# A two-layer decoder trunk in f32: new order of the first product and of the work at the boundaries between sublayers

## The chip, the cores and the metric

The kernel runs on one core of one Trainium2 chip. The metric is the device time of one execution in microseconds, the median of several runs.

## The reference

The input h is a residual stream of 256 tokens by 1024 channels in float32. Each of two layers computes, in this order (all weights float32):

```
f = swiglu(rms(h) @ ffn1_w_gu) @ ffn1_w_down;  h += 0.5 * rms(f)
u = rms(h) @ w_in                 # 5120 columns: q, k, v of two mixers, and two gates
h += rms((sigmoid(g1) * (stick_breaking(u) @ w1) + sigmoid(g2) * (differential(u) @ w2)) @ w_out)
f = swiglu(rms(h) @ ffn2_w_gu) @ ffn2_w_down;  h += 0.5 * rms(f)
e = (p[i] @ w_ple_proj) * sigmoid(rms(h) @ w_ple_gate);  h += rms(e)
```

rms(...) is a norm over the channels with a gain of its own each time. The hidden width of the FFNs is 2816; p[i] is 256 tokens by 256. The output has float32 accuracy, so each product is made of several reduced-precision ones.

## The kernel before, in words

**Units and splits.** The weights come in units of 2048 columns by 128 rows (1 MB). A unit is two halves of 1024 columns or four quarters of 512. `raw`, `w_hi` and `w_lo` hold three units each (three slots, unit u in slot u mod 3). SP loads a unit into `raw` as soon as VectorE has split the unit that was there. ScalarE rounds it to the fast format, with the norm's gain (`high`, line 646, also 643 and 657: `w_hi`). VectorE takes the rest (`low`, line 1084, also 1081, 1062, 1065 and in quarters 1098: `w_lo`). Every product is then three matmuls (`exact`, lines 1473 to 1475): high x high, low weights, low inputs. The inputs are split the same way: TensorE turns 128 tokens by 512 channels of h into a PSUM bank (`turn`, line 1520, four transposes), ScalarE copies the high part (`high_inputs`, line 677), VectorE the low part (`low_inputs`, line 1109).

**Tiles and order.** Tokens come in two tiles of 128 (t = 0, 1). `by_tiles` works two units in the order: unit u tile 0, unit u+1 tile 0, unit u tile 1, unit u+1 tile 1. A turn is put between two quarters of such a product; `before` is a table of what goes in front of quarter k. In `wide` products a quarter is 128 input channels by 512 output columns. In `deep` products quarter (n, k) is output columns n and input channels k, so the order over a unit's quarters is 0, 2, 1, 3.

**Boundaries.** Three times per layer (`boundary`, q = 1 before w_in, q = 3 before the second FFN, q = 4 before the gate) the last product of a sublayer ends, its squares are summed by ScalarE (`square_post`, line 694), GpSimd makes 1/sqrt of the mean (line 536 and `r_post`, line 538), VectorE multiplies by the gain (`gained`, line 1185) and adds to h (`update_h`, line 1198), each tile by halves of 512 channels. h is then turned and split for the next product. Beside this, both engines split the units that are used next: `next_unit` is unit u+1 of the coming pair, `unit_after` is unit u+2. All engines execute in order, so what stands ahead of a wait and what stands behind it is set by these two functions, one for ScalarE and one for VectorE. At the boundary TensorE first works unit u for tile 0, then the first quarter of unit u+1 for tile 0, then turns the first half of h's tile 1, then goes on; the turn of the second half stands in unit u for tile 1. Before unit u+1 it waits for all of the unit (`begin`).

**The opening.** The first product is p times the projection (unit 0), four pieces of 256 KB. Pieces 1 and 3 are loaded by SP, pieces 0 and 2 by ScalarE's queue, which then loads two quarters of x; the two others (indices 1 and 3) are issued by ScalarE between its splits (`load_x`). SP's queue begins with p's tile 0, piece 1, p's tile 1, piece 3, and then the pieces of units 1 to 3. TensorE runs 13 transposes of the identity (`warm_up`, line 1884), turns p's tile 0 (line 1877), runs 5 more, and begins `proj`.

Of the kernel before, what the change touches and what calls it, by code (L numbers as in the profile page):

```python
# [60 lines left out]
PIECED = 4  # L61
WARM_UP = (13, 5)
MEANS = 20
# [13 lines left out]
def trunk_kernel(nc, a, out):  # L77
    with ExitStack() as ctx:
# [9 lines left out]
        def bank(b):  # L88
            return ps[:, b, :]
# [257 lines left out]

        def p_bank(i):
            return bank(P_BANK if i else FIRST_P_BANK).rearrange("p (k n) -> p k n", k=2)

# [267 lines left out]
        def _(act):  # L618
# [41 lines left out]
            def high_p(i, t=0, toks=slice(0, SEQ)):  # L660

                act.wait_ge(p_turned, nth_p(i, t))
                act.activation(p_hi[:, :, toks], p_bank(i)[:, :, toks], ACT.Copy).then_inc(p_high, 1)

# [32 lines left out]
            def boundary(i, n, q, pairs, next_unit, unit_after):  # L697


                square_post(i, n, pair(pairs[0]), 0)  # L700
                next_unit(0)
                high_inputs(i, q, 0)
                next_unit(1)
                square_post(i, n, pair(pairs[1]), 1)
                unit_after()
                high_inputs(i, q, 1, (0,))
                square_pre(i, n + 1, 0)
                high_inputs(i, q, 1, (1,))
                square_pre(i, n + 1, 1)
# [216 lines left out]
            for i in range(DEPTH):  # L926
                def loads():
                    load_post(i, "ffn1_post_g", 0, 0)
                    load_post(i, "mix_post_g", 0, 1)
                    if i == 0:  # L930
# [7 lines left out]
                boundary(i, 0, 1, DOWN_PAIR,  # L938
                         lambda n: high(i, U_WIN + 1, 12, halves=(n,)), lambda: high(i, U_WIN + 2, 8))

# [5 lines left out]
                boundary(i, 1, 3, OUT_PAIR,  # L946
                         lambda n: high(i, U_FFN2 + 1, 20, halves=(n,)), lambda: high(i, U_FFN2 + 2, 16))

# [8 lines left out]
                if i < LAST:  # L957
                    high_p(i + 1)
                boundary(i, 2, 4, DOWN_PAIR,
                         lambda n: high(i, U_GATE + 1, 26, ks=2, halves=(n,)), lambda: high(i, U_GATE + 2, 28, ks=2))  # L960
                high(i, U_GATE + 3, 30, ks=2)
# [55 lines left out]
        def _(dve):  # L1017
# [351 lines left out]
            def low_p(i, t=0, toks=slice(0, SEQ)):  # L1369

                dve.wait_ge(p_high, nth_p(i, t))
                dve.tensor_tensor(p_lo[:, :, toks], p_bank(i)[:, :, toks], p_hi[:, :, toks].bitcast(F32),
                                  ALU.subtract).then_inc(p_split, 1)

            low_piece(U_PROJ, 0)
            low_p(0, 0, slice(0, P))
            low_piece(U_PROJ, 1)
            low_piece(U_PROJ, 2)
            low_p(0, 1, slice(P, SEQ))
            low_piece(U_PROJ, 3)  # L1380
            keep_first_gain()
# [88 lines left out]
        def _(pe):  # L1470
# [104 lines left out]
            def ffn(i, f, q, u0, before_last):  # L1575
# [85 lines left out]
                if (i, f) == (0, 0):  # L1661
                    for s in range(2):
                        for t in range(TT):
                            before = turned_at(0, 0, (1, 3)[t:t + 1], (1,)) if s == 0 else {}
                            if t == 0:
                                before = {k: pieced(u0 + s, k, before.get(k)) for k in range(4)}
                            mm = first_gate_up(s, t, before)
                            if s == 1 and t == 0:
                                mm.then_inc(gu_done, 1)
                        mm.then_inc(units_used, 1)  # L1670
                else:
                    second = turned_at(i, q, (2,), (1,))
                    if q == 0:
                        second[0] = lambda: pe.wait_ge(half_split, i)
                        second[2] = lambda: begin(i, u0 + 1)
                    by_tiles(i, u0, first_gate_up, gu_done, {(1, 0): second, (0, 1): turned_at(i, q, (3,), (1,))},
                             own_wait=(1,) if q == 0 else ())
                step(1, 1, first=True)
# [141 lines left out]
            def mixer(i):  # L1820
# [7 lines left out]
                def w_out(u, s, t, before):  # L1828
# [3 lines left out]

                by_tiles(i, U_WIN, first_win, win_done, {(1, 0): turned_at(i, 1, (2,), (1,)),
                                                         (0, 1): turned_at(i, 1, (3,), (1,))})
                for m in range(2, 20):
# [37 lines left out]
            def turn_p(i, tiles=range(TT)):  # L1873
                pe.wait_ge(p_in[tiles[0]], 16 * i + 16)
                for k in range(2):
                    for t in tiles:
                        mm = pe.transpose(p_bank(i)[:, k, t * P:(t + 1) * P], p_nat[:, t, k * P:(k + 1) * P],
                                          ident[:, :])
                mm.then_inc(p_turned, 1)
# [11 lines left out]
            def turn_gains():  # L1891
# [4 lines left out]
                pe.transpose(bank(GAIN_BANK[1])[:, 0:66], g_rows[0:66, :], ident[0:66, 0:66]).then_inc(cols_turned, 1)  # L1896

            def proj(i):

                if i:  # L1900
                    begin(i, U_PROJ)
                for t in range(TT):
                    pe.wait_ge(p_split, nth_p(i, t))
                    if i:
                        pe.wait_ge(ple_sig, 2 * i - 1 + t)
                        before = turned_at(i, 0, (0, 1), (1, 2)) if t == 0 else None
                    elif t == 0:
                        turns = {1: lambda: turn_p(0, (1,)), **turned_at(0, 0, (0,), (3,))}
                        before = {k: pieced(U_PROJ, k, turns.get(k)) for k in range(4)}
                    else:  # L1910
                        before = {0: turn_first_gain, **turned_at(0, 0, (2,), (2,)), 3: turn_gains}
# [7 lines left out]
            turn_p(0, (0,))  # L1919
            warm_up(WARM_UP[1])  # L1920
            for i in range(DEPTH):
                proj(i)
                ffn(i, 0, 0, U_FFN1, lambda: None)
# [4 lines left out]
                def gate(u, s, t, before):  # L1928
# [4 lines left out]
                by_tiles(i, U_GATE, lambda s, t, before: gate(0, s, t, before), None,  # L1933
                         {(1, 0): turned_at(i, 4, (2,), (1,)), (0, 1): turned_at(i, 4, (3,), (2,))})
                by_tiles(i, U_GATE + 2, lambda s, t, before: gate(2, s, t, before))
# [23 lines left out]
```

## Time and profile before

| | before |
|---|---|
| runs, us | 1187.34, 1187.6, 1187.7 (median 1187.6) |
| profiled execution, us | 1187.24 |
| its span, us | 1185.2 |
| TensorE matmul busy | 1173.8 us, 99% |
| VectorE, ScalarE, GpSimd busy | 72%, 61%, 8% |
| loaded from memory | 215 MB, 182 GB/s over the span |
| mean granted TensorE clock | 0.999 |

The span runs from the first to the last instruction; the execution's own time lies 2.0 us above it. Busy times of TensorE overlap, since a matmul's start is given exactly and its end is modelled: two matmuls of 512 columns start 0.23 us apart and are shown with 0.39 us each. So a gap of TensorE is best read from the starts. A row of the timeline gives start, duration, engine, line, operation, output and inputs, shape and count, and in brackets the idle time before it and what ended that.

### The profile page before, as it was taken

What the parts mean: (1) busy time and instruction counts of PE and PEld (TensorE: products, weight loads), DVE (VectorE), ACT (ScalarE), POOL (GpSimd) and SP (SyncE); (2) the same over time, 40 slices, a digit from 0 to 9 for tenths busy, and PEclk for the clock granted to TensorE, in tenths of its full rate; (3) what the DMA queues carried; (4) which work ended last, traced back from release to release, by engine and by line L of the source; (5) the groups of instructions that cost most, each with busy time, mean ns of one, the idle gap of its engine ahead of it and who ended that gap; (6) DMA issues with size and microseconds to landing.
All of it is one profiled execution on the core that took longest, in us unless ns stands there. A gap on an engine that the chain in (4) does not pass through costs nothing.

```text
span 1185.2 us, 17137 instructions
## 1 busy us (share of the span) xinstructions
PE 1173.8 (99%) x6013; PEld 984.4 (83%) x6013; DVE 848.7 (72%) x1235; ACT 719.9 (61%) x1163; POOL 92.9 (8%) x157
## 2 busy tenths in 40 slices
PE   8999999999999999999999999999999999999997
PEld 7888888888788888888888888888877888888886
DVE  5766777588667866676787776676976776767666
ACT  6655556666665755564685655576656666555555
POOL 4000000042000100000110000010600010000002
PEclk9999999999999999999999999999999999999999
DMA  8656565553345555556546565756343456556550
GB/s 269 232 183 201 171 218 192 198 178 118 132 178 178 178 196 194 191 172 230 178 158 203 175 209 178 249 162 208 114 159 133 169 178 213 175 179 206 183 196 36
DMA packets 138654, 215.36 MB, mean 182 GB/s; under 512 B 6958, under 2 KB 97904, under 8 KB 138608
## 3 DMA queue, kind: packets, MB, share of 16 engines
q1 hardware_dynamic: 135808, 208.43, 52.9%
q10 hardware_dynamic: 2576, 6.29, 1.6%
q8 instruction: 28, 0.46, 0.2%
q14 instruction: 18, 0.15, 0.0%
q0 software_dynamic: 224, 0.04, 0.0%
HBM read 213.68 MB, written 1.05 MB: 181 GB/s over the span
## 4 chain that ended last, share of the span: by engine, by line
PE 96%; ACT 2%; DVE 1%; DMA 1%; issue 0%; POOL 0%; SPq 0%; DVEq 0%; POOLq 0%; ACTq 0%
PE ps L1591 22%; PE ps L1473 19%; PE ps L1475 19%; PE ps L1474 19%; PE ps L1601 12%; PE ps L1520 2%; PE ps L1692 1%; DMA raw<-in_w_ple_proj 1%; PE ps L1723 1%; DVE w_lo L1084 0%; ACT w_hi L646 0%; PE ps L1736 0%; PE ps L1709 0%; ACT prob L804 0%; PE ps L1752 0%
## 5 line engine op out<-in xcount | busy, mean ns | idle before, releaser
L1084 DVE SCALAR_TENSOR_TENSOR w_lo<-raw,g_layer,w_hi 128x512 fp32r<-128x512 f32 (+1 forms) x504 | 369.6, 793 | 131.4 <-ACT w_hi L646 131.4
L646 ACT ACTIVATE w_hi<-raw,g_layer 128x512 fp32r<-128x512 f32 (+1 forms) x524 | 346.9, 732 | 113.5 <-PE ps L1601 97.0
L1591 PE MATMUL ps<-x_both,w_hi 128*128 128x512 f32 x1152 | 287.7, 392 | 0.0
L1473 PE MATMUL ps<-w_hi,x_both 128*128 128x512 f32 x640 | 257.4, 402 | 0.0
L1475 PE MATMUL ps<-w_hi,x_both 128*128 128x512 f32 x640 | 250.2, 391 | 0.0
L1474 PE MATMUL ps<-w_lo,x_both 128*128 128x512 f32 x640 | 249.6, 390 | 0.0
L1591 PEld LDWEIGHTS ps<-x_both,w_hi 128*128 128x128 f32 x1152 | 209.4, 189 | 39.3 <-issue 0.3
L1081 DVE TENSOR_TENSOR w_lo<-raw,w_hi 128x1024 fp32r<-128x1024 f32 x114 | 134.7, 1221 | 55.0 <-ACT w_hi L643 55.0
L643 ACT ACTIVATE w_hi<-raw 128x1024 fp32r<-128x1024 f32 x114 | 114.7, 1052 | 91.7 <-PE ps L1475 91.6
L1601 PEld LDWEIGHTS ps<-x_both,w_lo 128*128 128x128 f32 x1152 | 152.6, 191 | 8.4
L1601 PE MATMUL ps<-x_both,w_lo 128*128 128x256 f32 x1152 | 156.0, 283 | 0.0
L1473 PEld LDWEIGHTS ps<-w_hi,x_both 128*128 128x128 f32 x640 | 120.2, 188 | 27.1 <-issue 3.3
L1475 PEld LDWEIGHTS ps<-w_hi,x_both 128*128 128x128 f32 x640 | 120.1, 188 | 26.1
L1474 PEld LDWEIGHTS ps<-w_lo,x_both 128*128 128x128 f32 x640 | 120.4, 188 | 22.8
L1473 PE MATMUL ps<-w_hi,ht_hi 128*128 128x512 f32 x320 | 124.9, 390 | 0.0
L1475 PE MATMUL ps<-w_hi,ht_lo 128*128 128x512 f32 x320 | 124.6, 389 | 0.0
L1474 PE MATMUL ps<-w_lo,ht_hi 128*128 128x512 f32 x320 | 124.5, 389 | 0.0
L728 ACT ACTIVATE glu<-glu 128x512 f32<-128x512 f32 x36 | 22.8, 633 | 78.5 <-DVE glu L1130 78.5
L1475 PEld LDWEIGHTS ps<-w_hi,ht_lo 128*128 128x128 f32 x320 | 60.1, 188 | 12.5
L1474 PEld LDWEIGHTS ps<-w_lo,ht_hi 128*128 128x128 f32 x320 | 60.1, 188 | 12.4
L1473 PEld LDWEIGHTS ps<-w_hi,ht_hi 128*128 128x128 f32 x320 | 60.1, 188 | 12.3
L536 POOL TENSOR_TENSOR ms_post<-mean_post,eps_half 128x1 f32<-128x1 f32 x8 | 2.4, 305 | 548.6 <-ACT tmp L694 548.6
(217 smaller groups left out, 1008.7 us busy)
## 6 DMA issues: line engine op xcount, KB each, us to landing
raw<-in_ffn_w_gu SPq DMA_DIRECT2D x170, 512.0 KB, 4.6
raw<-in_ffn_w_down SPq DMA_DIRECT2D x88, 512.0 KB, 4.0
raw<-in_w_in SPq DMA_DIRECT2D x80, 512.0 KB, 4.6
raw<-in_w_out SPq DMA_DIRECT2D x16, 512.0 KB, 3.7
raw<-in_w_ple_gate SPq DMA_DIRECT2D x16, 512.0 KB, 4.1
raw<-in_w_branch_sb SPq DMA_DIRECT2D x8, 512.0 KB, 3.7
raw<-in_w_branch_diff SPq DMA_DIRECT2D x8, 512.0 KB, 3.7
raw<-in_ffn_w_gu SPq DMA_DIRECT2D x12, 256.0 KB, 7.6
```

The costliest lines, as they stand in the source:

```text
L643: last = act.activation(w_hi[:, s, part], raw[:, s, part], ACT.Copy)
L646: last = act.activation(w_hi[:, s, part], raw[:, s, part], ACT.Copy, scale=g_layer[:, g:g + 1])
L728: act.activation(glu_g, glu_g, ACT.Silu).then_inc(silu_done, 2)
L1081: last = dve.tensor_tensor(w_lo[:, s, part], raw[:, s, part], whi[:, part], ALU.subtract)
L1084: last = dve.scalar_tensor_tensor(out=w_lo[:, s, part], in0=raw[:, s, part], scalar=g_layer[:, g:g + 1], in1=whi[:, part], op0=ALU.mult, o ...
L1473: pe.matmul(dst, x_h, w_h, start=first, stop=False, **group)
L1474: pe.matmul(dst, x_h, w_l, start=False, stop=False, **group)
L1475: return pe.matmul(dst, x_l, w_h, start=False, stop=last, **group)
L1520: mm = pe.transpose(x_bank(i, q, idx)[:, k * P:(k + 1) * P], src[:, (4 * n + k) * P:(4 * n + k + 1) * P], ident[:, :])
L1591: mm = pe.matmul(dst, w_hi[:, s, cols], x_both[:, :, 4 * half + k, :], start=half == 0 and k == 0, stop=stop and k == 3, skip_group_check= ...
L1601: mm = pe.matmul(bank(FLAT_BANK[j])[:, 0:SEQ], w_lo[:, s, cols], x_hi[:, 4 * half + k, :], start=False, stop=False, skip_group_check=True)
L1692: mm = pe.transpose(dst[:, k * SEQ + t * P:k * SEQ + (t + 1) * P], src[:, t, k * P:(k + 1) * P], ident[:, :])
```

## The change

It has two parts.

In the opening, p's tile 1 is loaded second on SP's queue. TensorE turns both tiles of p before the first product, with 3 transposes in place of 5 between them, and each tile has a PSUM bank of its own. The product goes through the pieces in the order 0, 2 for tile 0, 0, 2 for tile 1, then 1, 3 and 1, 3; ScalarE and VectorE split in the order piece 0, p's tile 0, piece 2, p's tile 1, piece 1, piece 3.

At the three boundaries, ScalarE sums the squares of tile 1 ahead of the second half of `next_unit`, and does `unit_after` by halves. VectorE updates the first half of tile 1 of h ahead of the last two quarters of `next_unit`, and the second half of h behind the low part of the first half of x. Where the product is `deep` (ks = 2), the quarters of `next_unit` are split in the order 0, 2, 1, 3. TensorE waits for the first two split quarters before unit u+1 and for the rest before its third quarter.

```diff
-WARM_UP = (13, 5)
+WARM_UP = (13, 3)
...
-        HT_BANK, P_BANK, FIRST_P_BANK = 6, 7, 3
+        HT_BANK, P_BANK, FIRST_P_BANK = 6, 7, (3, 5)
...
-            load_p(0)
+            for t in range(TT):
+                load_p(t)
...
-            load_pieces(U_PROJ, (1,))
-            load_p(1)
-            load_pieces(U_PROJ, (3,))
+            load_pieces(U_PROJ, (1, 3))
...
@@ ScalarE, boundary @@
                 next_unit(0)
                 high_inputs(i, q, 0)
+                square_post(i, n, pair(pairs[1]), 1)
                 next_unit(1)
-                square_post(i, n, pair(pairs[1]), 1)
-                unit_after()
+                unit_after(0)
                 high_inputs(i, q, 1, (0,))
                 square_pre(i, n + 1, 0)
+                unit_after(1)
                 high_inputs(i, q, 1, (1,))
                 square_pre(i, n + 1, 1)
...
@@ ScalarE, opening @@
             high_p(0, 0, slice(0, P))
+            high_piece(U_PROJ, 2)
+            high_p(0, 1, slice(P, SEQ))
             high_piece(U_PROJ, 1)
-            high_p(0, 1, slice(P, SEQ))
-            high_piece(U_PROJ, 2)
             high_piece(U_PROJ, 3)
             load_x(1)
...
@@ VectorE @@
-            def low_quarter(i, u, gain, ks, k):
-
+            def low_quarter(i, u, gain, ks, n):
+
+                k = n if ks == 4 else (0, 2, 1, 3)[n]
                 s, part = slot(u), slice(k * W, (k + 1) * W)
-                if k % 2 == 0:
-                    dve.wait_ge(hi_ready, 2 * UNITS * i + 2 * u + k // 2 + 1)
+                dve.wait_ge(hi_ready, 2 * UNITS * i + 2 * u + k // 2 + 1)
...
-                if k == 3:
+                if n == 1:
+                    ins.then_inc(half_split, 1)
+                if n == 3:
                     ins.then_inc(split_done, 1)
...
                 for k in range(2):
                     next_unit(k)
                     low_inputs(i, q, 0, (k,))
+                wait_gained(i, n, 1)
+                gained(i, n, pair(pairs[1]), 1, 0)
+                update_h(i, n, 1, 0)
                 for k in range(2, 4):
                     next_unit(k)
-                wait_gained(i, n, 1)
-                for k in range(2):
-                    gained(i, n, pair(pairs[1]), 1, k)
-                    update_h(i, n, 1, k)
+                gained(i, n, pair(pairs[1]), 1, 1)
                 low_inputs(i, q, 1, (0,))
+                update_h(i, n, 1, 1)
                 unit_after()
                 low_inputs(i, q, 1, (1,))
...
@@ TensorE @@
+            def by_halves(i, q, u, second):
+
+                second[0] = lambda: pe.wait_ge(half_split, 4 * i + (0, 1, None, 2, 3)[q])
+                second[2] = lambda: begin(i, u + 1)
+                return second
...
+            def first_proj():
+
+                beside = {(0, 1): lambda: (turn(0, 0, 0), turn_first_gain()), (0, 3): lambda: turn(0, 0, 2),
+                          (1, 3): turn_gains}
+                for t, k in ((0, 0), (0, 2), (1, 0), (1, 2), (0, 1), (0, 3), (1, 1), (1, 3)):
+                    if (t, k) in beside:
+                        beside[t, k]()
+                    if k == 0:
+                        pe.wait_ge(p_split, nth_p(0, t))
+                    if t == 0 and k < 3:
+                        pe.wait_ge(piece_split, (0, 2, 1).index(k) + 1)
+                    if (t, k) == (0, 3):
+                        begin(0, U_PROJ)
...
             warm_up(WARM_UP[0])
             turn_p(0, (0,))
             warm_up(WARM_UP[1])
+            turn_p(0, (1,))
+            first_proj()
             for i in range(DEPTH):
-                proj(i)
+                if i:
+                    proj(i)
```

## Rows read from the trace of the kernel before

**Rows 1.** The page, chain of work that ended last, by engine.

```profile
PE 96%; ACT 2%; DVE 1%; DMA 1%; issue 0%; POOL 0%; SPq 0%; DVEq 0%; POOLq 0%; ACTq 0%
```

**Rows 2.** Waits, TensorE's weight loads: us in total, times, longest.

```profile
PEld ps L1520 <- DVE h L1198: 3.1, 11, 0.4
```

**Rows 3.** Timeline, TensorE at the boundary to the second FFN: start, us, what.

```profile
384.93 0.40 PE L1475 MATMUL ps<-w_hi,x_both 128*128 128x512 f32 x1
...
388.35 0.39 PE L1475 MATMUL ps<-w_hi,x_both 128*128 128x512 f32 x1
388.76 0.66 PE L1520 MATMUL ps<-ident,h 128*128 128x128 f32 x4
...
394.56 0.39 PE L1473 MATMUL ps<-w_hi,x_both 128*128 128x512 f32 x1
```

**Rows 4.** Timeline, TensorE at the boundary to the gate.

```profile
570.73 0.39 PE L1475 MATMUL ps<-w_hi,x_both 128*128 128x512 f32 x1
...
573.70 0.39 PE L1473 MATMUL ps<-w_hi,x_both 128*128 128x512 f32 x1
...
574.38 0.65 PE L1520 MATMUL ps<-ident,h 128*128 128x128 f32 x4
```

**Rows 5.** Windows: stretch, its length, busy PE, PEld, DVE, ACT, POOL, clock, DMA, GB/s.

```profile
5.50:10.00 4.50, 2.80 (x13) 1.56 (x12) 2.14 (x4) 2.00 (x4) 3.17 (x17) 1.00 1.04 333
```

**Rows 6.** DMA issues at 0.80, 1.25, 1.72, 2.19 and 9.54: us to landing last.

```profile
soft<-in_p SPq DMA_DIRECT2D x1, 128.0 KB, 2.9
...
raw<-in_w_ple_proj ACTq DMA_DIRECT2D x1, 256.0 KB, 5.1
...
soft<-in_p SPq DMA_DIRECT2D x1, 128.0 KB, 5.5
...
raw<-in_w_ple_proj SPq DMA_DIRECT2D x1, 256.0 KB, 7.3
...
h<-in_x ACTq DMA_DIRECT2D x1, 256.0 KB, 5.8
```

**Rows 7.** Timeline, ScalarE in the opening, projection piece 3.

```profile
9.54 0.63 ACT L657 ACTIVATE w_hi<-raw 128x512 fp32r<-128x512 f32 x1 [0.68 <-DMA raw<-in_w_ple_proj]
```

**Rows 8.** Timeline, TensorE in the opening.

```profile
1.59 3.04 PE L1884 MATMUL ps<-ident 128*128 128x128 f32 x13 [1.59 <-POOL ident L474]
...
5.99 0.50 PE L1473 MATMUL ps<-w_hi,p_hi 128*128 128x512 f32 x1
...
6.55 0.40 PE L1475 MATMUL ps<-w_hi,p_lo 128*128 128x512 f32 x1
...
15.92 0.39 PE L1473 MATMUL ps<-w_hi,x_both 128*128 128x512 f32 x1
...
16.61 0.60 PE L1520 MATMUL ps<-ident,h 128*128 128x128 f32 x4
```

**Rows 9.** Timeline, VectorE, ScalarE and GpSimd at the boundary to the second FFN.

```profile
385.82 1.41 DVE L1098 SCALAR_TENSOR_TENSOR w_lo<-raw,g_layer,w_hi 128x512 fp32r<-128x512 f32 x2
...
387.95 0.75 DVE L1198 SCALAR_TENSOR_TENSOR h<-tmp,r_post,h 128x512 f32<-128x512 f32 x1
...
393.34 0.69 DVE L1109 TENSOR_TENSOR x_both<-ps,x_both 128x512 fp32r<-128x512 f32 x1
...
385.69 1.02 ACT L694 ACTIVATE tmp<-ps 128x1024 f32<-128x1024 f32 x1
386.59 0.20 ACT L694 ACTIVATION_READ_ACCUMULATOR tmp<-ps 128x1 f32 x1
...
387.36 0.56 POOL L538 TENSOR_TENSOR r_post<-ms_post,neg_half 128x1 f32<-128x1 f32 x1
```

**Rows 10.** Timeline, VectorE and ScalarE at the boundary to the gate.

```profile
570.12 0.75 DVE L1098 SCALAR_TENSOR_TENSOR w_lo<-raw,g_layer,w_hi 128x512 fp32r<-128x512 f32 x1
...
570.26 1.14 ACT L646 ACTIVATE w_hi<-raw,g_layer 128x1024 fp32r<-128x1024 f32 x1
571.31 1.01 ACT L694 ACTIVATE tmp<-ps 128x1024 f32<-128x1024 f32 x1
```

More of the change, by code:

```diff
@@ L346, in trunk_kernel, with p_bank @@
         X_FIRST_BANK = (0, 0, 1, 1)
-        def p_bank(i):
-            return bank(P_BANK if i else FIRST_P_BANK).rearrange("p (k n) -> p k n", k=2)
+        def p_bank(i, t=0):
+            return bank(P_BANK if i else FIRST_P_BANK[t]).rearrange("p (k n) -> p k n", k=2)
         def nth_p(i, t):
@@ L662, in high_p @@
                 act.wait_ge(p_turned, nth_p(i, t))
-                act.activation(p_hi[:, :, toks], p_bank(i)[:, :, toks], ACT.Copy).then_inc(p_high, 1)
+                act.activation(p_hi[:, :, toks], p_bank(i, t)[:, :, toks], ACT.Copy).then_inc(p_high, 1)
             def keep_e(i, t):
@@ L938, in _ @@
                 boundary(i, 0, 1, DOWN_PAIR,
-                         lambda n: high(i, U_WIN + 1, 12, halves=(n,)), lambda: high(i, U_WIN + 2, 8))
+                         lambda n: high(i, U_WIN + 1, 12, halves=(n,)), lambda n: high(i, U_WIN + 2, 8, halves=(n,)))
                 load_post(i, "ffn2_post_g", 1, 0)
@@ L946, in _ @@
                 boundary(i, 1, 3, OUT_PAIR,
-                         lambda n: high(i, U_FFN2 + 1, 20, halves=(n,)), lambda: high(i, U_FFN2 + 2, 16))
+                         lambda n: high(i, U_FFN2 + 1, 20, halves=(n,)),
+                         lambda n: high(i, U_FFN2 + 2, 16, halves=(n,)))
                 act.preload_act_table_set("silu_and_others")
@@ L959, in _ @@
                 boundary(i, 2, 4, DOWN_PAIR,
-                         lambda n: high(i, U_GATE + 1, 26, ks=2, halves=(n,)), lambda: high(i, U_GATE + 2, 28, ks=2))
+                         lambda n: high(i, U_GATE + 1, 26, ks=2, halves=(n,)),
+                         lambda n: high(i, U_GATE + 2, 28, ks=2, halves=(n,)))
                 high(i, U_GATE + 3, 30, ks=2)
@@ L1371, in low_p @@
                 dve.wait_ge(p_high, nth_p(i, t))
-                dve.tensor_tensor(p_lo[:, :, toks], p_bank(i)[:, :, toks], p_hi[:, :, toks].bitcast(F32),
+                dve.tensor_tensor(p_lo[:, :, toks], p_bank(i, t)[:, :, toks], p_hi[:, :, toks].bitcast(F32),
                                   ALU.subtract).then_inc(p_split, 1)
@@ L1376, in _ @@
             low_p(0, 0, slice(0, P))
-            low_piece(U_PROJ, 1)
             low_piece(U_PROJ, 2)
             low_p(0, 1, slice(P, SEQ))
+            low_piece(U_PROJ, 1)
             low_piece(U_PROJ, 3)
@@ L1671, in ffn @@
                 else:
[L1672 to L1675, printed above, removed]
+                    second = by_halves(i, q, u0, turned_at(i, q, (2,), (1,)))
                     by_tiles(i, u0, first_gate_up, gu_done, {(1, 0): second, (0, 1): turned_at(i, q, (3,), (1,))},
-                             own_wait=(1,) if q == 0 else ())
+                             own_wait=(1,))
                 step(1, 1, first=True)
@@ L1831, in w_out @@
                                 u + s == 0, u + s == 3, before)
-                by_tiles(i, U_WIN, first_win, win_done, {(1, 0): turned_at(i, 1, (2,), (1,)),
-                                                         (0, 1): turned_at(i, 1, (3,), (1,))})
+                by_tiles(i, U_WIN, first_win, win_done, {(1, 0): by_halves(i, 1, U_WIN, turned_at(i, 1, (2,), (1,))),
+                                                         (0, 1): turned_at(i, 1, (3,), (1,))}, own_wait=(1,))
                 for m in range(2, 20):
@@ L1876, in turn_p @@
                     for t in tiles:
-                        mm = pe.transpose(p_bank(i)[:, k, t * P:(t + 1) * P], p_nat[:, t, k * P:(k + 1) * P],
+                        mm = pe.transpose(p_bank(i, t)[:, k, t * P:(t + 1) * P], p_nat[:, t, k * P:(k + 1) * P],
                                           ident[:, :])
@@ L1896, in turn_gains @@
                 pe.transpose(bank(GAIN_BANK[1])[:, 0:66], g_rows[0:66, :], ident[0:66, 0:66]).then_inc(cols_turned, 1)
+            def first_proj():
[10 more added lines that the diff above has]
+                        begin(0, U_PROJ)
+                    cols, toks = piece(U_PROJ, k), slice(t * P, (t + 1) * P)
+                    mm = exact(bank(E_PAIR[t] + k // 2), p_hi[:, k % 2, toks], p_lo[:, k % 2, toks],
+                               w_hi[:, slot(U_PROJ), cols], w_lo[:, slot(U_PROJ), cols], k % 2 == 0, k % 2 == 1)
+                    if (t, k) == (0, 3):
+                        mm.then_inc(e_done, 1)
+                mm.then_inc(units_used, 1)
             def proj(i):
-                if i:
-                    begin(i, U_PROJ)
+                begin(i, U_PROJ)
                 for t in range(TT):
                     pe.wait_ge(p_split, nth_p(i, t))
[L1904 to L1911, printed above, removed]
+                    pe.wait_ge(ple_sig, 2 * i - 1 + t)
+                    before = turned_at(i, 0, (0, 1), (1, 2)) if t == 0 else None
                     mm = deep(slot(U_PROJ), E_PAIR[t], p_hi, p_lo, 0, t, True, True, before)
@@ L1933, in _ @@
                 by_tiles(i, U_GATE, lambda s, t, before: gate(0, s, t, before), None,
-                         {(1, 0): turned_at(i, 4, (2,), (1,)), (0, 1): turned_at(i, 4, (3,), (2,))})
+                         {(1, 0): by_halves(i, 4, U_GATE, turned_at(i, 4, (2,), (1,))),
+                          (0, 1): turned_at(i, 4, (3,), (2,))}, own_wait=(1,))
                 by_tiles(i, U_GATE + 2, lambda s, t, before: gate(2, s, t, before))
```

## The prediction

> **What bounds the kernel now.** I read the page first: TensorE's matmuls hold 96% of the chain that ended last, all other engines together 4% [rows 1]. So an edit is worth only what it does to TensorE's gaps. The list of waits says how little there is to win at the boundaries: the transposes of h (L1520) waited 3.1 us in all over 11 cases, on the weight-load side, where the matmul before hides part of it [rows 2]. The array itself loses less. From 384.93 to 388.35 it makes 15 matmuls, 0.228 us apart; the turn of h then starts at 388.76, 0.41 later, so 0.18 us is lost, and some 0.06 more for restarting [rows 3]. At the gate boundary the turn comes 0.23 x 3 behind 573.70, so only the restart is lost [rows 4]. Four boundaries of the first kind and two of the second hold at most 4 x 0.24 + 2 x 0.07 = 1.1 us. The opening holds more: between 5.5 and 10 us TensorE is busy for 2.80 us of 4.50 [rows 5].
>
> The profiled execution is 1187.24 us around a span of 1185.2; the median of the three runs is 1187.6, so I add 0.36 at the end. A difference under 0.2% (2.4 us) can't be told from none.
>
> **The opening.** Removed: two warm-up transposes. Moved: p's second load from third to second place on SP's queue, so projection piece 1 goes behind it; piece 2's split ahead of piece 1's on ScalarE and VectorE; TensorE turns p's tile 1 before any product and then works pieces 0 and 2 for both tiles before 1 and 3. No instruction is added.
> Landings: p's first tile lands 2.9 us after its issue at 0.80, the second 5.5 after 1.72 (7.2); piece 2 5.1 after 1.25 (6.4), piece 3 7.3 after 2.19 (9.5), x's second half 5.8 after 9.54 (15.3) [rows 6]. p's tile 1 will be issued at 1.26. It lands no earlier than the first (3.7) and no later than its old time, with more bytes ahead (7.2); it's nearest to the first, 128 KB behind it, so I take 4.5. TensorE reaches it at 5.4, behind 13 warm-ups, p's tile 0 and 3 more, in the place of the two that go. Piece 1 takes p's old place in the bytes, 7.2.
> Chain: ScalarE splits piece 2 at 6.4 (0.63 us a piece), p's tile 1 (about 0.4) at 7.0, piece 1 at 7.3, piece 3 at 9.54 as now, since DMA sets that one [rows 7]; VectorE follows each with 0.69, what it needs for another 128x512 subtraction [rows 9]: piece 2 done at 7.8, p at 8.1, piece 1 at 8.8, piece 3 at 10.9 as now. TensorE: first product at 5.99 as now [rows 8], wait to 7.8, then three quarters of three matmuls (0.23 each, 0.69) to 10.0; x's first turn (0.35) and the gain's; quarter 1 from 10.55, another turn, quarter 3 at 11.7 (its weights 10.9, not late), quarters 1 and 3 of tile 1, end 14.0. Now the first matmul on x starts at 15.92 [rows 8]: 1.9 us earlier.
> What is late next: the turn of x's second half. TensorE comes to it at 14.0 + 0.69 = 14.7, and the data land at 15.3, because ScalarE issues that load behind piece 3's split, which hasn't moved. Now this turn stands at 16.61 [rows 8]; it will stand at 15.4. So 0.7 of the 1.9 us turns into a new wait and **the opening gives 1.2 us**. Behind it ScalarE's and VectorE's splits follow TensorE's turns and shift with them. Bounds: 0.4 (piece 2 or p's tile 1 late by 0.8) to 1.9 (the load no hindrance).
> The clock: the first 13 warm-ups take 3.04 us, 0.23 each; x's four transposes later take 0.60, 0.15 each [rows 8]. So the array was at the lower of its two levels (1.2 GHz) at first, at 2.4 later, and as many transposes stand before the first product after the change as now: I price this at 0. The Trainium skill, TensorE: Matmul & The Clock Gate, Part 4 (PE-mode transpose), says that a transpose doesn't count as activity that brings the full clock. By that rule the products would open at the low clock, before and after alike, for the same sum. The trace disagrees: behind transposes alone, the first product takes 0.56 us from its first matmul at 5.99 to its third at 6.55, two steps that at half the rate would take 0.9 [rows 8].
>
> **The four wide boundaries** (to w_in and to the second gate-up, twice each; same code and shapes). I work out the one at 388. ScalarE now squares tile 1 (385.69) behind the second half of the next unit's split. Squaring moves ahead of that half, but it waits for TensorE's last product, whose last matmul starts at 384.93 and lasts 0.40 [rows 3]: it starts at 385.4, and 1.1 us later the squares are there, 386.5 against 386.79. GpSimd adds 1.13, to r_post's end: 387.6 against 387.92 [rows 9]. h's first half gets its update (0.75) at 387.65, done 388.4, and TensorE's turn goes at 388.58 without a gap: 0.24 gained.
> The price is VectorE's order. Today it fills the time until the squares are there with quarters 2 and 3 (385.82, 1.41 us) [rows 9]. After the change these stand behind the update, so it idles from 385.8 to 386.5 and, with one 0.68 product between, from 387.2 to 387.65. Then: quarters 2 and 3 to 389.75, against TensorE's need at 389.7 (0.09 lost); product 0.68; x's low part of tile 1, first half, done 391.0, needed 391.2; update of h's second half 391.7, needed 391.9; both just in time. Then the whole of the unit after (four quarters, 2.65 us with overlap) to 394.25, and only behind it the low part of tile 1's second half, done 394.95, now 393.34 + 0.69 = 394.03 [rows 9]. TensorE needs it where it now starts that product, 394.56 [rows 3], less 0.24 plus 0.09 = 394.4. That is a new stall of 0.55 us. **Net +0.4 each, +1.7 in all.** The split of the unit after is not halved on VectorE, so ScalarE's halving buys nothing. Bounds: -0.24 (no stall) to +0.9 (all of the lateness).
>
> **The two gate boundaries.** There the product wants quarters 0 and 2 first, and the new order of the quarters gives it them. But quarter 2 lies in the second half of the unit, whose high part ScalarE now makes behind the squares. Before: half at 570.26 (1.14 us), squares at 571.31 [rows 10]. After: the squares wait for the last matmul (570.73 + 0.39 [rows 4]), start 571.18, the next instruction 0.99 later: half from 572.17 to 573.3. VectorE, in order, has quarter 2 where quarter 1 stands at 570.12 [rows 10], at the head of its queue; it idles until 573.35, and behind it stand x's low part, product and update of tile 1. Quarter 2 is done at 574.1 (0.75), TensorE wants it at 573.70 [rows 4]: 0.45 lost. Then x's low part (0.62 step), product (0.72), update (0.75) end at 576.1: the turn goes at 576.2 instead of 574.38. Then quarters 1 and 3 end at 577.5, wanted at 577.4. From there VectorE has everything in time. **+1.9 to +2.0 each, +3.9 in all.** Lower bound -0.07, no stall; upper +2.6, should the low part of tile 1 also come late.
> Later stages: the unit after is split, by the same counting, about 3 us ahead of its need. Its slots in raw come free up to 5 us later, and SP's loads behind them; each has the whole of two units' products, some 11 us, to land in 4 to 5. TensorE has no idle time further on that could absorb the shift, so it is carried to the end.
>
> **Sum.** -1.2 + 1.7 + 3.9 = +4.4 us on 1187.24: 1191.6, with 0.36 for the median 1192.0.
>
> **The rivals.**
> (a) As above, 70%: own range 1190.4 to 1193.4.
> (b) The wide boundaries don't stall, because the ten steps of VectorE between 385.8 and 394.95 are 0.55 us shorter than I add them up. Then 4 x -0.24 instead of +1.7: 1189.3. Against it: each step is read from a row, and all would have to be 6% short. 14%.
> (c) The clock, place: 5.4 to 6 us. If p's tile 1 still lands near 7.2, TensorE idles in front of the first product with two warm-ups fewer, and the products start at the low clock: 24 matmuls at 0.43 (512 columns at half the rate of 0.228) are 4.8 us more, less what waits hide, some 3: 1195. For it: the old landing; against: fewer bytes ahead. The page above would have the low clock without late data. 4%.
> (d) Faster: the gate unit's second half isn't late. It decides at VectorE's quarter 2: were the half high by 571.4 as now, quarter 2, product and update would fit before 574.4; and if likewise at the wide boundaries, with nothing lost to the order, all 1.1 is gained and the opening's 1.2 to 1.9: 1184.6 to 1185.3. The order written out for ScalarE speaks against it. 5%.
> (e) The change doesn't do what it says in the opening: a late piece eats the 1.2, so 1193.2. 7%.
>
> **How the numbers follow.** (a) and (b) are 84%; the range from 1189.2 to 1193.8 takes in both and (e). Slower by over 0.2% begins at 1190.0: all of (a), (c), (e) and a bit of (b): 0.82. Faster, under 1185.2: 0.04. The rest 0.14.
>
> **What would show it.** TensorE's list of waits gets entries on VectorE's low part of x at four boundaries (0.5 each), and at two gates on h's update (1.3 each) and on quarter 2 (0.45 each); ScalarE's second half of the gate unit starts behind the squares; the first matmul on x stands near 14.0, and the turn behind it waits for the load of x. I'm wrong if TensorE shows no idle of a microsecond near 575, or if the opening's turn of x's second half goes before 15.

## The result and the profile after

The changed kernel takes 1191.18 us (median of 8 runs, 1190.6 to 1191.48) beside 1187.39 us for the kernel before (8 runs): the ratio is 1.0031, 95% interval 1.002 to 1.0042. It is slower by 3.8 us. The profiled execution took 1191.3 us around a span of 1189.2, which is 4.0 more than before, so its trace can be read for nearly the whole difference of the medians.

The page of the changed kernel, chain of work that ended last, by engine:

```profile
PE 92%; DVE 4%; ACT 2%; DMA 1%; issue 1%; POOL 0%; SPq 0%; DVEq 0%; POOLq 0%; ACTq 0%
```

In [rows 1] VectorE had 1% of this chain and TensorE 96%. The chain now leaves TensorE more often. The waits of the changed kernel say where, first TensorE's matmuls, then its weight loads (us in total, times, longest; the line of a turn is now L1525, that of the first of three matmuls L1478):

```profile
PE ps L1525 <- DVE h L1202: 2.1, 2, 1.0
...
PE ps L1525 <- DMA h<-in_x: 1.6, 1, 1.6
PE ps L1478 <- DVE w_lo L1100: 0.8, 2, 0.4
PE ps L1478 <- DVE x_both L1113: 0.7, 4, 0.2
...
PEld ps L1525 <- DVE h L1202: 3.8, 7, 1.5
...
PEld ps L1478 <- DVE x_both L1113: 2.4, 4, 0.6
```

The first four lines are the waits of the matmuls: two waits on h's update (the gates), one on the load of x (the opening), two on a split quarter (the gates), four on the low part of x (the wide boundaries). None of them was in the matmuls' list of before. In [rows 2] the weight loads' waits on h were 11 short ones; here 2 of the 7 make up most of the sum.

To see how much each cost, I set the starts of the same turns in both traces side by side. A turn's shift is its start after minus its start before, and the step is the shift less that of the row above. So the step of a row is what the stretch between the two turns cost; the cost of a boundary, which falls behind its first turn, stands in the row below it. (In the opening, "x's second half" is channels 512 to 1023 of tile 0, and "x's last half" the same channels of tile 1.)

| turn | start before | shift | step |
|---|---|---|---|
| x's second half, in the opening | 16.61 | -1.10 | -1.10 |
| first turn at the boundary to w_in | 198.17 | -1.05 | +0.05 |
| first turn at the boundary to FFN 2 | 382.20 | -0.80 | +0.25 |
| first turn at the gate boundary | 568.00 | -0.57 | +0.23 |
| first turn behind the gate, layer 1 | 594.43 | +1.54 | +2.11 |
| boundary to w_in, layer 2 | 782.65 | +1.56 | +0.02 |
| boundary to FFN 2, layer 2 | 966.66 | +1.79 | +0.23 |
| gate boundary, layer 2 | 1151.99 | +2.01 | +0.22 |
| last turn of that boundary | 1162.30 | +4.10 | +2.09 |

So the opening gave 1.05, each wide boundary cost 0.22 to 0.25, each gate 2.1, and everything between them next to nothing: -1.05 + 0.93 + 4.20 = +4.1.

**The gate.** Timeline of the changed kernel: ScalarE, then VectorE, then TensorE, to be set beside [rows 4, 10]:

```profile
570.60 1.03 ACT L693 ACTIVATE tmp<-ps 128x1024 f32<-128x1024 f32 x1 [0.79 <-PE ps L1480]
571.52 0.19 ACT L693 ACTIVATION_READ_ACCUMULATOR tmp<-ps 128x1 f32 x1
571.61 2.18 ACT L645 ACTIVATE w_hi<-raw,g_layer 128x1024 fp32r<-128x1024 f32 x2
...
572.79 0.75 DVE L1100 SCALAR_TENSOR_TENSOR w_lo<-raw,g_layer,w_hi 128x512 fp32r<-128x512 f32 x1 [3.15 <-ACT w_hi L645]
573.46 0.68 DVE L1113 TENSOR_TENSOR x_both<-ps,x_both 128x512 fp32r<-128x512 f32 x1
574.06 0.68 DVE L1189 TENSOR_TENSOR tmp<-ps,post_g 128x512 f32<-128x512 f32 x1
574.84 0.75 DVE L1202 SCALAR_TENSOR_TENSOR h<-tmp,r_post,h 128x512 f32<-128x512 f32 x1
...
573.68 0.47 PE L1478 MATMUL ps<-w_hi,x_both 128*128 128x512 f32 x1 [0.40 <-DVE w_lo L1100]
...
575.65 0.66 PE L1525 MATMUL ps<-ident,h 128*128 128x128 f32 x4 [1.03 <-DVE h L1202]
```

ScalarE idles 0.79 us for TensorE's last product, sums the squares and only then makes the second half (571.61). In VectorE's order nothing stands ahead of quarter 2 that it could do, so it idles 3.15 us; the three steps queued behind it end at 575.6, and the turn of h goes 0.06 later. The last matmul before the turn had started at 574.22.

**A wide boundary** (to the second FFN), VectorE, GpSimd, TensorE of the changed kernel, beside [rows 3, 9]. This boundary starts 0.80 us earlier than before:

```profile
385.77 0.69 DVE L1189 TENSOR_TENSOR tmp<-ps,post_g 128x512 f32<-128x512 f32 x1 [0.81 <-ACT tmp L693]
386.60 0.75 DVE L1202 SCALAR_TENSOR_TENSOR h<-tmp,r_post,h 128x512 f32<-128x512 f32 x1
387.27 1.41 DVE L1100 SCALAR_TENSOR_TENSOR w_lo<-raw,g_layer,w_hi 128x512 fp32r<-128x512 f32 x2
...
390.45 2.73 DVE L1086 SCALAR_TENSOR_TENSOR w_lo<-raw,g_layer,w_hi 128x512 fp32r<-128x512 f32 x4
393.11 0.68 DVE L1113 TENSOR_TENSOR x_both<-ps,x_both 128x512 fp32r<-128x512 f32 x1
...
385.74 0.19 POOL L535 TENSOR_TENSOR ms_post<-mean_post,eps_norm 128x1 f32<-128x1 f32 x1 [5.54 <-ACT tmp L693]
386.01 0.55 POOL L537 TENSOR_TENSOR r_post<-ms_post,neg_half 128x1 f32<-128x1 f32 x1
...
387.55 0.39 PE L1480 MATMUL ps<-w_hi,x_both 128*128 128x512 f32 x1
387.78 0.60 PE L1525 MATMUL ps<-ident,h 128*128 128x128 f32 x4
...
393.28 0.39 PE L1480 MATMUL ps<-w_hi,x_both 128*128 128x512 f32 x1
393.85 0.50 PE L1478 MATMUL ps<-w_hi,x_both 128*128 128x512 f32 x1 [0.18 <-DVE x_both L1113]
```

The turn now follows the matmul by the usual 0.23 (387.55 to 387.78), where it was 0.41. But the low part of x starts at 393.11, behind four quarters of the unit after, ends at 393.79, and TensorE's step from 393.28 to 393.85 is 0.57, 0.34 too long, with some 0.1 more for restarting.

**The opening**, TensorE and ScalarE of the changed kernel, beside [rows 7, 8]:

```profile
5.82 0.50 PE L1478 MATMUL ps<-w_hi,p_hi 128*128 128x512 f32 x1 [0.39 <-DVE p_lo L1377]
...
13.10 0.39 PE L1478 MATMUL ps<-w_hi,x_both 128*128 128x512 f32 x1
...
15.51 0.63 PE L1525 MATMUL ps<-ident,h 128*128 128x128 f32 x4 [1.57 <-DMA h<-in_x]
...
5.20 0.62 ACT L656 ACTIVATE w_hi<-raw 128x512 fp32r<-128x512 f32 x1
...
9.34 0.63 ACT L656 ACTIVATE w_hi<-raw 128x512 fp32r<-128x512 f32 x1 [1.46 <-DMA raw<-in_w_ple_proj]
9.35 0.34 ACTq L623 DMA_DIRECT2D h<-in_x  x1
```

The first matmul on x stands at 13.10, 2.8 us earlier than before, and then TensorE waits for x's second half: 1.7 of the 2.8 are lost there.

### The profile page after: what moved, and what is told of

Its sections match the earlier page's. It is cut to its first block, busy times and chain, and to the rows that moved or that the text cites. A ratio compares the mean times of both kernels' runs of the same rounds, so it can differ in the third digit from the quotient of the medians.

```text
span 1189.2 us, 17131 instructions
## 1 busy us (share of the span) xinstructions
PE 1174.5 (99%) x6011; PEld 983.7 (83%) x6011; DVE 847.8 (71%) x1235; ACT 720.2 (61%) x1163; POOL 91.8 (8%) x157
## 3 DMA queue, kind: packets, MB, share of 16 engines
HBM read 213.68 MB, written 1.05 MB: 181 GB/s over the span
## 4 chain that ended last, share of the span: by engine, by line
PE 92%; DVE 4%; ACT 2%; DMA 1%; issue 1%; POOL 0%; SPq 0%; DVEq 0%; POOLq 0%; ACTq 0%
PE ps L1602 22%; PE ps L1478 18%; PE ps L1480 17%; PE ps L1479 17%; PE ps L1612 12%; DVE w_lo L1086 1%; PE ps L1525 1%; PE ps L1700 1%; DVE h L1202 1%; ACT w_hi L645 1%; DMA raw<-in_w_ple_proj 1%; PE ps L1731 1%; DVE x_both L1113 1%; DMA h<-in_x 1%; DVE w_lo L1100 0%
## 5 line engine op out<-in xcount | busy, mean ns | idle before, releaser
L1478 PE MATMUL ps<-w_hi,x_both 128*128 128x512 f32 x640 | 258.2, 403 | 1.5 <-DVE w_lo L1100 0.8
L1478 PEld LDWEIGHTS ps<-w_hi,x_both 128*128 128x128 f32 x640 | 120.2, 188 | 31.8 <-issue 4.9
L1478 PE MATMUL ps<-w_hi,ht_hi 128*128 128x512 f32 x320 | 124.9, 390 | 0.0
L1478 PEld LDWEIGHTS ps<-w_hi,ht_hi 128*128 128x128 f32 x320 | 60.1, 188 | 12.3
L1136 DVE TENSOR_TENSOR glu<-glu,prob 128x512 f32<-128x512 f32 x36 | 24.9, 693 | 27.6 <-ACT glu L728 27.6
```

Source lines behind the costliest of these rows:

```text
L1136: dve.tensor_tensor(glu_g, glu_g, wide_r, ALU.mult).then_inc(silu_scaled, 1)
L1478: pe.matmul(dst, x_h, w_h, start=first, stop=False, **group)
```

## The experiments

The kernels ran in three groups, each with the kernel before on the same chip (1187.36, 1187.25 and 1187.54 us). Where kernels of different groups are compared, the distance of each from its own kernel before counts. Shifts of turns are against the trace before, as in the table above.

### The two parts alone

The first takes the opening's edits alone, the second the boundaries' alone.

> The kernel before with the opening of the change alone; the boundaries as before. Theory: the two parts add up, and the opening alone is worth what the turn of x's second half gained (16.61 to 15.51 us), so the span is 1.1 us below before (1184.1) and the turns of h at all boundaries stand 1.1 us earlier. Rival: the early start is given back at the first boundaries, as DMA or the splits run behind; then the turns near 205 and 388 are as before and the span is 1185.2.

Measured: 1186.26 us against 1187.36, ratio 0.999 (0.998 to 0.9999), so 1.1 us faster in the median, as expected. The profiled execution was the slowest of the ten: its span is 1184.8, not 1184.1, and that is the load of x again. In this execution piece 3 landed later:

```profile
10.02 0.63 ACT L656 ACTIVATE w_hi<-raw 128x512 fp32r<-128x512 f32 x1 [1.68 <-DMA raw<-in_w_ple_proj]
10.02 0.33 ACTq L623 DMA_DIRECT2D h<-in_x  x1
```

The load of x is issued behind it, and the turn stands at 16.29, 6.27 behind the issue. All later turns, to the last, keep the shift of that one (-0.32, then -0.25 to -0.33). So the rival, that the early start is given back at the first boundaries, falls: what is gained at the first turns stays.

> The kernel before with the boundaries of the change alone; the opening as before. Theory: the loss of the six boundaries does not depend on the opening: 4 x 0.23 + 2 x 2.09 = 5.1 us, span 1190.3. Rival: some of the loss is there only because the work arrives earlier; then the span is nearer to 1189.

Measured: 1192.5 us against 1187.36, ratio 1.0044 (1.0028 to 1.0061), span 1190.1. The boundaries cost 5.1 us in the median (4.9 in the span) also without the early opening, and the two parts add up within the noise: -1.1 + 5.1 = +4.0, beside the +3.8 measured for the whole change.

### The gates: ScalarE's half, or the order of the quarters

```diff
@@ ScalarE, boundary @@
+                if q == 4:
+                    next_unit(1)
                 square_post(i, n, pair(pairs[1]), 1)
-                next_unit(1)
+                if q != 4:
+                    next_unit(1)
                 unit_after(0)
```

> The changed kernel, but at the two gate boundaries ScalarE makes the second half of the next unit ahead of tile 1's squares, as before. Theory: the gates' 2.1 us each come from VectorE standing at quarter 2 for that half (572.8), so TensorE's waits on quarter 2 (0.4 each) and on h (1.0 and more each) go and the span falls by 4.2 to 1185.0. Rival: the order of VectorE's own work (the update behind the quarter and the low part) holds TensorE, whatever ScalarE does; then at most the 0.5 of quarter 2 goes, twice: 1188.2.

Measured: 1187.47 us, 3.7 below the changed kernel (ratio to before 1.0002, 0.9992 to 1.0011), span 1185.1. The shift across the first gate boundary is from -0.92 to -0.73, 0.2 instead of 2.1. VectorE, ScalarE and TensorE at the first gate of this kernel:

```profile
570.52 0.75 DVE L1103 SCALAR_TENSOR_TENSOR w_lo<-raw,g_layer,w_hi 128x512 fp32r<-128x512 f32 x1 [1.21 <-ACT w_hi L645]
...
572.58 0.75 DVE L1205 SCALAR_TENSOR_TENSOR h<-tmp,r_post,h 128x512 f32<-128x512 f32 x1
...
569.35 1.14 ACT L645 ACTIVATE w_hi<-raw,g_layer 128x1024 fp32r<-128x1024 f32 x1
570.39 1.02 ACT L693 ACTIVATE tmp<-ps 128x1024 f32<-128x1024 f32 x1
...
573.47 0.60 PE L1528 MATMUL ps<-ident,h 128*128 128x128 f32 x4
```

VectorE still waits at quarter 2, but 1.21 us and not 3.15, and neither quarter 2 nor the turn of h is late any more. The 0.2 that is left is lost later: quarters 1 and 3 still stand behind the update and end at 574.66, and TensorE starts on them at 574.71, 0.34 behind the matmul before, with one longer step behind it (0.34). VectorE's own order is the same as in the changed kernel, so it isn't the cause of the 2.1 by itself.

The other way round: ScalarE as in the change, the quarters in plain order, TensorE waiting for the whole unit.

```diff
-                k = n if ks == 4 else (0, 2, 1, 3)[n]
+                k = n
...
@@ TensorE, gate @@
-                         {(1, 0): by_halves(i, 4, U_GATE, turned_at(i, 4, (2,), (1,))),
-                          (0, 1): turned_at(i, 4, (3,), (2,))}, own_wait=(1,))
+                         {(1, 0): turned_at(i, 4, (2,), (1,)),
+                          (0, 1): turned_at(i, 4, (3,), (2,))})
```

> The changed kernel, but at the gate VectorE splits the quarters in the plain order 0, 1, 2, 3 and TensorE waits for the whole unit before it, as before the change; ScalarE still sums the squares first. It tells whether the order of quarters or that of ScalarE is to blame. Theory: VectorE no longer stands at quarter 2, but quarters 2 and 3 are now behind tile 1's update, so the whole unit is split near 574.9, wanted near 573.1: the loss at the gates stays about 1.9 each, moved from the turn of h to the unit: span 1188.8. Rival: the new order of the quarters is the cause by itself; then the gates cost at most 0.3 each: 1185.6.

Measured: 1190.5 us against 1187.25 (ratio 1.0026, 1.0016 to 1.0036), span 1188.2. The shift across the gates is from -0.74 to +0.99 and from +1.40 to +3.11, 1.7 each. The wait has moved, as TensorE's list of waits in this kernel says:

```profile
PE ps L1478 <- DVE w_lo L1100: 3.0, 2, 1.5
```

The timeline of TensorE in the same kernel, at the first gate, has one of the two:

```profile
574.61 0.50 PE L1478 MATMUL ps<-w_hi,x_both 128*128 128x512 f32 x1 [1.48 <-DVE w_lo L1100]
```

The rival (at most 0.3 a gate) falls. Either way, something that TensorE wants at 573 stands behind the squares: the half that ScalarE makes, or the two quarters that VectorE put behind the update. The new order of the quarters costs 0.4 us a gate more than the plain one beside ScalarE's new order (2.1 against 1.7), and at most 0.2 beside ScalarE's old order.

### The wide boundaries: the unit after by halves

```diff
@@ VectorE, boundary @@
                 update_h(i, n, 1, 1)
-                unit_after()
+                unit_after((0,))
+                if q == 4:
+                    unit_after((1,))
                 low_inputs(i, q, 1, (1,))
+                if q != 4:
+                    unit_after((1,))
...
```

> The changed kernel, but at the four wide boundaries VectorE splits only the first half of the unit after ahead of the low part of tile 1's second half, and the second half behind it. Theory: TensorE's wait on that low part (0.33 to 0.37 from the starts, and 0.1 for restarting) goes at each, 4 x 0.45 = 1.8 us: span 1187.4, with 0.2 a boundary better than before the change. Rival: the low part waits for ScalarE's high part, which follows TensorE's turn at 390.99 us; then it comes no earlier than 392.3, in time as well; or the second half of the unit after becomes late and the time stays at 1189.

Measured: 1189.27 us, 1.9 below the changed kernel (ratio to before 1.0017, 1.0007 to 1.0027), span 1187.2. VectorE at the boundary to the second FFN in this kernel:

```profile
389.93 1.41 DVE L1086 SCALAR_TENSOR_TENSOR w_lo<-raw,g_layer,w_hi 128x512 fp32r<-128x512 f32 x2
391.70 0.69 DVE L1113 TENSOR_TENSOR x_both<-ps,x_both 128x512 fp32r<-128x512 f32 x1 [0.36 <-ACT x_both L676]
392.31 1.41 DVE L1086 SCALAR_TENSOR_TENSOR w_lo<-raw,g_layer,w_hi 128x512 fp32r<-128x512 f32 x2
```

The low part starts 1.26 us behind the turn of that half (390.44) and not 2.12, waits 0.36 for ScalarE's high part (so far the rival is right, and it doesn't matter), and TensorE's wait on x_both is gone from its list. The shifts across the first two wide boundaries are -1.10 to -1.34 and -1.34 to -1.61: 0.24 and 0.27 gained, where the change lost 0.25 and 0.23. The gates stay at +2.1.

### The opening: the load of x earlier

```diff
             high_piece(U_PROJ, 2)
+            load_x(1)
             high_p(0, 1, slice(P, SEQ))
             high_piece(U_PROJ, 1)
             high_piece(U_PROJ, 3)
-            load_x(1)
```

> The changed kernel, but ScalarE issues the load of x's second half behind the split of piece 2 (near 5.2 us) and not behind that of piece 3 (near 9.3). Theory: this load alone holds the turn of x's second half in the opening (in four runs the turn stood 6.1 to 6.3 us behind that issue); it then lands before 13 us and the turn goes at 13.8 instead of 15.5: span 1187.5, 1.7 below the changed kernel. Rival: the DMA engines are full until 16 us, so this load pushes the pieces behind it and TensorE waits for weights of units 1 or for the next turn instead; then the turn of x's last half (18.8) moves by under 0.8 us.

Measured: 1191.38 us against 1187.25 (ratio 1.0034, 1.0023 to 1.0045): no better than the changed kernel. The profiled execution, 1190.52 us around a span of 1188.4, was the second fastest of its eight. In it the first turn goes at once, and the next one waits. The first product's matmuls are shown with them:

```profile
5.98 0.79 PE L1478 MATMUL ps<-w_hi,p_hi 128*128 128x512 f32 x1
6.57 0.63 PE L1479 MATMUL ps<-w_lo,p_hi 128*128 128x512 f32 x1
7.00 0.52 PE L1480 MATMUL ps<-w_hi,p_lo 128*128 128x512 f32 x1
...
14.30 0.60 PE L1525 MATMUL ps<-ident,h 128*128 128x128 f32 x4
...
17.94 0.63 PE L1525 MATMUL ps<-ident,h 128*128 128x128 f32 x4 [0.28 <-DMA h<-in_x]
```

The turn of x's second half moved from 15.51 to 14.30, that of the last from 18.77 to 17.94: 0.8 is kept, at the edge of what the rival allowed. The last load is issued at 11.72 here, behind the gains. So this run alone settles that the next load takes over as the bound.

The 14.30 (13.8 were expected) has another cause than a load: x's second half had landed at 12.0 (6.9 us behind its issue at 5.09), and TensorE itself came late. Its first products start 0.59 and 0.43 us apart here; in the trace of the changed kernel above, it was 0.33 and 0.23 (5.82, 6.15, 6.38). A step of 0.43 for 512 columns is the lower of the two levels (1.2 GHz), although the profile's clock column says 1.00 for this stretch. The first matmul on x starts at 13.62, where it was 13.10. Of the nine profiles with the new opening, six begin the first product at the lower level (first matmul on x at 13.48 to 13.80) and three don't (13.10 to 13.23), with the same 20 transposes ahead. With the loads of x where the change has them, this lateness disappears in the wait for the load; with the load early, it shows.

### All corrections, and what each is worth over many executions

One kernel has both boundary corrections and both late loads of x earlier (the second half behind piece 2, the last behind piece 3); it ran twice. Another has the boundary corrections alone, a third those with the opening of before.

> The changed kernel with both loads of x early (behind pieces 2 and 3), the second half of the gate unit ahead of the squares, and the unit after split by halves on VectorE at the wide boundaries. Theory: the three corrections add up: -1.7 or more, -4.2, -1.8 from 1189.2, span 1181.5, faster than before by 3.7 us. Rival: the splits of ScalarE and VectorE in the first 25 us leave no room for a further 1.7 us; then 1183.

Measured: 1184.5 us against 1187.25, ratio 0.9975 (0.9965 to 0.9984), span 1182.3. That is 2.8 us faster than before, less than the 3.7 expected.

> The changed kernel with both boundary corrections (gate half ahead of the squares, unit after by halves on VectorE) and the loads of x where the change has them. Beside the kernel with all three corrections it tells what the early loads are worth over many executions, where the two profiles said 0.8 and the timed runs of the changed kernel nothing. Theory of additive parts: span 1189.2 - 4.2 - 1.8 = 1183.2, time near 1185.3. If the early loads bring something, the fully mended kernel is below this by 0.8 us in the medians; if not, the two medians agree within 0.3.

Measured: 1185.39 us against 1187.54, ratio 0.998 (0.9971 to 0.9989), span 1182.7.

> The kernel before with the boundaries of the change and both boundary corrections; the opening as before. Theory: the boundaries' waits of before (0.24 at four, 0.07 at two) are all there is to gain, so 1.0 us: span 1184.3, time near 1186.4. Rival: the new waits by halves cost something elsewhere, and it is no faster than before.

Measured: 1186.6 us against 1187.54, ratio 0.9994 (0.9985 to 1.0003), span 1184.8. The median is 0.9 us below before, but the interval includes no change at all. In the trace the four wide boundaries gain 0.21 to 0.28 each and the two gates lose 0.2 each.

> The same kernel as e6_all_mended, in the same call as the two others so that its median can be set beside theirs: 1184.5 again, with an interval that excludes no change.

Measured: 1184.32 us against 1187.54, ratio 0.9972 (0.9962 to 0.9983), span 1182.0. The list of what TensorE's matmuls waited for is down to this, and none of it is at a boundary:

```profile
PE ps L1899 <- POOL ident L473: 1.6, 1, 1.6
PE ps L1782 <- ACT mixed_t L816: 0.4, 2, 0.2
PE ps L1485 <- DVE p_lo L1384: 0.4, 1, 0.4
```

In one group of runs, the kernel with the early loads is 1.07 us below the one without (1184.32 and 1185.39). So with both loads early and the boundaries mended they are worth a microsecond over many executions; the earlier of them alone, with the boundaries of the change, brought nothing. This version beats both the kernel before and the changed one: it is 3.2 us under the first, in the same group.

## Why the prediction was right

Forecast were 1192.0 us, 1189.2 to 1193.8, and slower; measured 1191.18. The mechanism is the one that case (a) named, and the experiments that remove a cause at the boundaries remove its cost. Of the signs named ahead, the waits on h, on quarter 2 and on the low part of x appeared where forecast, and so did the wait for the load of x; the first matmul on x came at 13.10 and not near 14.0. Point by point, by the terms of the sum (+4.4 forecast, +4.0 in the span):

- **The gates, +1.9 to +2.0 each: measured 2.1.** Quarter 2 was forecast done 0.45 behind TensorE's need, the turn 1.8 late, and both are so: quarter 2 is done at 573.54, 0.42 behind need, and the turn starts at 575.65, 1.84 behind 574.38 less the 0.57 by which this boundary began earlier. What was short is the end: the wait for quarters 1 and 3 costs 0.13 and the restart behind it 0.11.
- **The wide boundaries, +0.4 each: measured +0.22 to +0.25.** The cause is right, the stall of 0.55 was sized too long; it measured 0.34 and a restart of 0.1 that the forecast left out. The step that was mis-sized is GpSimd's 1.13 us from the squares to r_post's end, carried over from [rows 9]. It took 0.90 here (squares there at 385.66, r_post at 386.56), since the sum took 0.19 and not 0.41. Nor did quarters 2 and 3 come 0.09 late.
- **The opening, -1.2: measured -1.05**, with an error ahead of the bound that the bound hides. Piece 2 landed at 5.05 and not at 6.4 (3.8 us behind its issue, where 5.1 was carried over from [rows 6]), and the product ended 0.9 earlier than forecast (first matmul on x at 13.10, forecast 14.0). All of that was lost at the load of x: forecast to land at 15.3, it was issued at 9.35, landed 6.0 us later and was used at 15.51. That the forecast of this term came out so near is owed to the bound, which was right; the chain ahead of it wasn't. Piece 3's landing sets the load's issue: in the profiles of the changed kernel, of its opening alone and of the four kernels that differ from the changed one only at the boundaries, the turn stood 6.1 to 6.3 us behind that issue, wherever it was (8.72 to 10.02).
- **Nothing further on absorbs or adds:** between the boundaries the shifts change by 0.02 to 0.05 us over 180 us. That TensorE's chain has no slack there fits with this, and it is why the terms could be added.
- **Rival (b)**, no stall at the wide boundaries, needed all of the 0.55 us gone; 0.2 of them were. **Rival (c)**, the clock: in the profile of the changed kernel its condition isn't met, since p's tile 1 had landed when TensorE came to it, and the first product runs at the higher level. But the lower level came without that condition, in six of the nine profiles with the new opening, and in one with the old: it then lasts for the first two or three matmuls (0.43 from start to start, as priced) and not for 24, and the first matmul on x comes 0.3 to 0.5 us later. The forecast had this at 0 from a single trace (what it read there, that the clock can rise behind transposes alone, holds in the trace of the changed kernel too: the 3 transposes at 4.72 start 0.11 apart, ahead of any product); that it doesn't show in the sum is owed to the load of x, which is waited for in any case. **Rival (d)** is near to what the kernel with the half ahead of the squares and the unit after by halves does: it is decided at VectorE's quarter 2, as said, and comes to 1185.39 and not 1184.6 to 1185.3. **Rival (e)** didn't occur in the profile shown, though the opening alone had an execution in which a late piece ate 0.8 of the gain.

Left open: why the early load alone showed 0.8 us in its profile and nothing in its median. Its executions spread over 1.7 us (1190.1 to 1191.84), those of the changed kernel over 0.9, which fits a bound set by landings. The profiled one was a fast one although its first product began at the lower level, so the level alone doesn't explain the slower ones; no run here shows what does.

## What to carry to other kernels

Where one engine has no slack, price a reordering by what stands behind each wait on the helpers' in-order queues. At a wide boundary the wait that the change removed was 0.24 us; at a gate the new wait, with the work queued behind it, cost 2.1. Before an engine gets a new wait near the head of its queue (quarter 2), look when the other engine will have produced what it waits for, in the new order of that engine, and halve on both sides or on none. A load that is issued behind another load's use inherits that one's landing; once everything around it is faster, it is the bound.

## What was not expected of the hardware

GpSimd's addition of one column (128x1) took 0.41 us before at this place and 0.19 after. In the lists by tile, the additions on ms_post of the two kinds shown took 191 to 421 ns before and all of 189 to 191 ns after:

```profile
L536 POOL TENSOR_TENSOR ms_post<-mean_post,eps_half x8: 191/304/421, 196.2 to 1156.5; 128x1 f32<-128x1 f32 x8
L536 POOL TENSOR_TENSOR ms_post<-mean_post,eps_norm x6: 191/192/415, 380.2 to 971.3; 128x1 f32<-128x1 f32 x6
```

```profile
L535 POOL TENSOR_TENSOR ms_post<-mean_post,eps_half x8: 189/189/189, 195.1 to 1158.4; 128x1 f32<-128x1 f32 x8
L535 POOL TENSOR_TENSOR ms_post<-mean_post,eps_norm x6: 189/190/191, 379.4 to 972.8; 128x1 f32<-128x1 f32 x6
```

(The first fence is the kernel before, the second the changed one; shortest, median, longest in ns.) Before, VectorE was splitting quarters beside it (385.82 to 387.23), an operation with two inputs in SBUF; after, it was idle or reading PSUM. The same holds over the whole trace of the kernel before: 13 of its 30 additions of this kind, those on ms_pre included, took 0.32 to 0.85 us, and each of the 13 ends about 0.05 us behind the end of such a VectorE operation that ran when it began. In the changed kernel 7 of 30 are slow. At the wide boundaries only those on ms_pre are still slow, now beside the update of h, which reads tmp and h from SBUF (389.79 to 390.53 at the second FFN; the addition runs from 390.12 to 390.58). In both traces the others took 0.19 us; a few of them began within 0.02 us of such an operation or in its last 0.15 us. The Trainium skill, SBUF — State Buffer, section "SBUF: two separate sides", says that a VectorE operation with two SBUF inputs and a GpSimd operation that reads SBUF can't run together, and that the later one waits. The traces agree in the slow cases of both kernels: each ends with the operation beside it. So GpSimd's part of a boundary got shorter by 0.2 us when the change took the quarters from beside it, which a sum from the rows before couldn't show.

Nor was it expected how much the landings vary. Piece 3's split in the changed opening began between 8.71 and 10.02 us in nine profiles, and where the load of x is issued behind it, a later landing is passed on to the whole: in the kernel with the opening alone it came 0.68 later than in the changed kernel, and the turn of x's second half 0.78.
